# The last tile of an encoder's router on one Trainium2 core: the norm ahead of the row picks, the picks in halves, and another place for the first picked rows

## The reference

```
x = x + concat[GLA(xn), Fourier(xn), MLA(xn)] @ w_out       # xn = rms_norm(x)
t = rms_norm(x)
group = top1(softmax(t @ w_rg + b_rg))                      # 4 groups
two experts = top2(softmax of the 8 logits of that group)   # t @ w_re + b_re, 32 experts
y = sum over the two: weight * (silu(t @ w_gate[e]) * (t @ w_up[e])) @ w_down[e]
return rms_norm(x + y)
```

## Time and profile before

| | |
|---|---|
| median of 3 runs | 531.3 us (530.68 to 532.53) |
| the profiled execution | 531.76 us, span 530.0 us |
| TensorE busy | 493.6 us, 93% of the span, mean granted clock 0.986 |
| VectorE busy | 210.1 us, 40% |
| ScalarE busy | 136.6 us, 26% |
| GpSimd busy | 75.2 us, 14% |
| DMA | 139.95 MB, mean 264 GB/s |
| the chain that ended last | PE 70%, DMA 11%, SPq 8%, DVE 7%, issue 2%, ACT 1% |

### The profile page before, as it was taken

How to read it: one execution, slowest core, us unless ns; L and a number is a source line. 1 busy time by engine, 2 the same in 40 slices (tenths; PEclk the granted TensorE clock), 3 DMA queues, 4 the chain that set the end, 5 groups by cost and what they waited for, 6 DMA issues and landing times.

```text
span 530.0 us, 7702 instructions
## 1 busy us (share of the span) xinstructions
PE 493.6 (93%) x2932; PEld 272.6 (51%) x2932; DVE 210.1 (40%) x561; ACT 136.6 (26%) x357; POOL 75.2 (14%) x101
## 2 busy tenths in 40 slices
PE   4999999999999999999999999999999878788993
PEld 3446544569755555445456555555555434444431
DVE  3217320663576770116763422332233202332166
ACT  4404211362476761203131111111111101111023
POOL 1000000344000000000213122222222212110100
PEclk9999999999999999999998999999999989998998
DMA  8996000010496004941089999999999999999974
GB/s 296 356 279 244 2 1 0 16 36 2 155 416 263 2 1 151 419 144 40 2 307 361 402 420 414 413 419 416 416 414 416 417 415 415 417 415 417 399 288 159
DMA packets 40134, 139.95 MB, mean 264 GB/s; under 512 B 9848, under 2 KB 12984, under 8 KB 31904
## 3 DMA queue, kind: packets, MB, share of 16 engines
q1 hardware_dynamic: 34752, 131.38, 63.1%
q0 software_dynamic: 4816, 7.85, 4.0%
q10 hardware_dynamic: 528, 0.22, 0.2%
HBM read 130.47 MB, written 16.39 MB: 277 GB/s over the span
## 4 chain that ended last, share of the span: by engine, by line
PE 70%; DMA 11%; SPq 8%; DVE 7%; issue 2%; ACT 1%; DVEq 0%; ACTq 0%
PE bank L1063 15%; PE bank L748 12%; DMA EW<-in_moe_w_up 9%; PE bank L928 9%; PE bank L1076 6%; SPq L616 5%; PE bank L911 4%; PE bank L974 3%; PE bank L963 2%; SPq L621 2%; PE bank L845 2%; PE bank L1036 2%; DMA EW<-in_w_in 2%; PE bank L884 1%; PE bank L756 1%
## 5 line engine op out<-in xcount | busy, mean ns | idle before, releaser
L1063 PE MATMUL bank<-EW,WO 128*64 128x256 f32 x640 | 78.3, 400 | 9.8 <-DMA EW<-in_moe_w_up 8.0
L1063 PEld LDWEIGHTS bank<-EW,WO 128*64 128x64 f32 x640 | 47.4, 144 | 35.6 <-DMA EW<-in_moe_w_up 8.8
L748 PE MATMUL bank<-EW,XT 128*128 128x512 f32 (+1 forms) x192 | 64.1, 495 | 0.0
L928 PE MATMUL bank<-WO,XT 128*128 128x512 f32 x128 | 56.6, 595 | 0.0
L1400 ACT ACTIVATE G<-bank 128x128 f32<-128x128 f32 x32 | 8.9, 277 | 178.5 <-PE bank L1063 169.3
L1763 DVE TENSOR_TENSOR G<-G,bank 128x128 f32<-128x128 f32 x32 | 9.2, 287 | 111.7 <-ACT G L1400 93.3
L1988 POOL DMA_INDIRECT y_scratch<-G,sidx x30 | 30.2, 1008 | 162.1 <-DVE G L1776 149.6
L748 PEld LDWEIGHTS bank<-EW,XT 128*128 128x128 f32 x192 | 32.9, 190 | 31.0 <-issue 31.0
L1776 DVE COPY G<-bank 128x512 f32<-128x512 f32 x32 | 22.1, 692 | 47.7 <-PE bank L1076 47.7
L1076 PE MATMUL bank<-EW,G 128*64 128x512 f32 x160 | 38.3, 599 | 0.0
L928 PEld LDWEIGHTS bank<-WO,XT 128*128 128x128 f32 x128 | 23.7, 190 | 27.3 <-issue 27.3
(11 more groups left out here) (291 smaller groups left out, 654.3 us busy)
## 6 DMA issues: line engine op xcount, KB each, us to landing
EW<-in_moe_w_gate SPq DMA_DIRECT2D x20, 1024.0 KB
EW<-in_moe_w_up SPq DMA_DIRECT2D x20, 1024.0 KB
EW<-in_moe_w_down SPq DMA_DIRECT2D x20, 1024.0 KB
y_scratch<-MIX SPq DMA_DIRECT2D x8, 512.0 KB, 9.1
WO<-in_w_out SPq DMA_DIRECT2D x2, 2048.0 KB, 11.7
MIX<-in_moe_w_gate SPq DMA_DIRECT2D x4, 1024.0 KB
MIX<-in_moe_w_up SPq DMA_DIRECT2D x4, 1024.0 KB
WO<-in_moe_w_gate SPq DMA_DIRECT2D x4, 1024.0 KB
```

The lines of the kernel that those rows point to most:

```text
L748: mm = pe.matmul(ps[:, 0:width], xnT[:, c, t * P:(t + 1) * P], w_in_sb[:, c, col:col + width], start=(c == 0), stop=(c == C - 1))
L928: mm = pe.matmul(ps[:, :], xnT[:, c, t * P:(t + 1) * P], w_out_sb[:, c, n * 512:(n + 1) * 512], start=(c == 0), stop=(c == C - 1))
L1063: mm = pe.matmul(bank[BLOCK * m:BLOCK * (m + 1), 0:2 * P].rearrange("p (w n) -> p w n", w=2), xeT[:, c, par * BLOCK:(par + 1) * BLOCK], wv ...
```

## The change

The order of the last steps changes: the norm of tile 3 goes ahead of its logits and of all picks, each pick is split into its two halves, the halves stand before and behind `("Lf", 3)`, `("L", 3)` and `("pos", 3)`. Both filler products are gone. Tile 2's list work leaves its `("pos", 2)` step: the rows are made inside the norm of tile 3, the places after it, and the weights after the selection of tile 3. The two places of gathered rows are exchanged, so that the first picked rows go to the last part of w_out and the first gathered pair to tile 2 of X; VectorE and ScalarE no longer wait for the stores of x. `pick_done` counts halves: VectorE waits for one, ScalarE, SyncE and the first gather for two.

```diff
--- before.py
+++ after.py
@@ -163,8 +163,9 @@
 
 OUT_ORDER = [("out", 0, 0), ("out", 0, 1), ("out", 1, 0), ("T", 0), ("norm", 0), ("out", 1, 1), ("Lf", 0),
              ("out", 2, 0), ("L", 0), ("T", 1), ("norm", 1), ("out", 2, 1), ("Lf", 1), ("pos", 0), ("T", 2), ("norm", 2),
-             ("L", 1), ("out", 3, 0), ("pos", 1), ("Lf", 2), ("L", 2), ("out", 3, 1), ("pos", 2), ("T", 3), ("pick", 0),
-             ("Lf", 3), ("norm", 3), ("L", 3), ("pick", 1), ("pick", 2), ("pos", 3), ("pick", 3)]
+             ("L", 1), ("out", 3, 0), ("pos", 1), ("Lf", 2), ("L", 2), ("out", 3, 1), ("pos", 2), ("T", 3), ("norm", 3), ("pick", 0, 0),
+             ("Lf", 3), ("L", 3), ("pick", 0, 1), ("pick", 1, 0), ("pick", 1, 1), ("pick", 2, 0), ("pos", 3),
+             ("pick", 2, 1), ("pick", 3, 0), ("pick", 3, 1)]
 
 
 def attention_order():
@@ -363,7 +364,7 @@
         hg = view(G, 3840, (2, P))
         hT = view(G, 4096, (2, 2, BLOCK))
 
-        xg = [X[:, 2, :], view(WO, 7168, (D,))]
+        xg = [view(WO, 7168, (D,)), X[:, 2, :]]
         ovx = MIX[:, 0, :]
         yzero = MIX[:, 3, 512:D]
         onehot_held = [MIX[:, i, 0:512].rearrange("p (t d s) -> p t d s", t=T, d=2) for i in range(2)]
@@ -650,7 +651,7 @@
             for t in range(T):
                 drained(sp, ("Lf", t))
             load_gate_up(RING + 2, RING + 2)
-            sp.wait_ge(pick_done, 1)
+            sp.wait_ge(pick_done, 2)
             sp.wait_ge(x2_stored, 16 * T)
             load_down(RING + 2, RING + 2)
             sp.wait_ge(weights_ready, 1)
@@ -728,10 +729,6 @@
                     mm = pe.transpose(banks[PLAN[("xT", c)][0]][:, t * P:(t + 1) * P], X[:, t, c:D:C], ident[:, :])
                     if t == T - 1:
                         close_bank(mm, ("xT", c))
-
-            def keep_busy(ps, data):
-
-                pe.matmul(ps[:, :], ident[:, :], data, start=True, stop=True)
 
             def by_feature(key, col, width):
 
@@ -1007,23 +1004,19 @@
                     ps = open_bank(step)
                     close_bank(pe.matmul(ps[:, 0:NG + NE], lf[t % 2], small[:, STACK:ONE_UP], start=True, stop=True), step)
                 elif kind == "pick":
-                    if t == T - 1:
-                        keep_busy(open_bank(("ids", 1)), X[:, 0, 0:512])
                     pe.wait_ge(sel_ready, 2 * t + 2)
                     drained(pe, ("out", t, 0))
                     drained(pe, ("out", t, 1))
+                    n = step[2]
                     if t == 0:
                         for i in range(T * MH - 3, T * MH):
                             drained(pe, ("S", i))
-                    for n in range(2):
-                        mm = pe.matmul(banks[n][:, :], sel0[:, t].rearrange("p e s -> p (e s)"),
-                                       X[:, t, n * 512:(n + 1) * 512], start=(t == 0), stop=(t == T - 1))
+                    mm = pe.matmul(banks[n][:, :], sel0[:, t].rearrange("p e s -> p (e s)"),
+                                   X[:, t, n * 512:(n + 1) * 512], start=(t == 0), stop=(t == T - 1))
                     if t == T - 1:
                         mm.then_inc(pick_done, 1)
                 elif kind == "pos":
                     ps = open_bank(step)
-                    if t == T - 1:
-                        keep_busy(ps, X[:, 0, 0:512])
                     pe.wait_ge(picks_ready, t + 1)
                     for u in range(t + 1):
                         mm = pe.matmul(ps[:, 0:NE], tri[:, 1 if u < t else 0, :], mska[:, u, :],
@@ -1381,8 +1374,7 @@
 
             act.preload_act_table_set("silu_and_others")
 
-            act.wait_ge(pick_done, 1)
-            act.wait_ge(x2_stored, 16 * T)
+            act.wait_ge(pick_done, 2)
             act.activation(xg[0][:, 512:D], banks[1][:, :], ACT.Copy).then_inc(picked, 1)
             def copy_half(half):
                 for j in range(4):
@@ -1665,6 +1657,28 @@
                 link(dve.reciprocal(wts[:, t, 0:1], sc[:, 8:9]))
                 return dve.tensor_tensor(wts[:, t, 1:2], wts[:, t, 0:1], sc[:, 4:5], ALU.mult)
 
+            def positions(t, ps):
+                link(dve.scalar_tensor_tensor(pos1[:, t], ps[:, 0:NE], 1.0, mska[:, t], ALU.add, ALU.mult))
+                for e in range(2):
+                    dve.tensor_scalar(sel0[:, t, e], slot_no[:, e], pos1[:, t, e:e + 1], rn2[:, t, 2:3],
+                                      ALU.is_equal, ALU.mult).then_inc(sel_ready, 1)
+                dve.tensor_tensor(sel4[:, t].rearrange("p (a u) s -> p a u s", u=2),
+                                  pos1[:, t, 2:6].rearrange("p (a u) -> p a u", u=2).unsqueeze(3).to_broadcast([P, 2, 2, BLOCK]),
+                                  slot_no.unsqueeze(1).to_broadcast([P, 2, 2, BLOCK]),
+                                  ALU.is_equal).then_inc(sel4_ready, 1)
+
+            def list_rows(t, ps):
+                step = ("pos", t)
+                row, rows2 = rt[:, t, 10], rt[:, t, 11:13]
+                free_bank(dve.tensor_tensor(row, ps[:, 0:NE], small[:, 0:NE], ALU.add), step)
+                drained(dve, step)
+                link(dve.tensor_tensor(rows2, oh[:, t], row.unsqueeze(1).to_broadcast([P, 2, NE]), ALU.mult))
+
+            def list_places(t):
+                link(dve.tensor_reduce(rt[:, t, 0, 10:12], rt[:, t, 11:13], AX, ALU.add))
+                dve.scalar_tensor_tensor(dest[:, t, :], rt[:, t, 0, 10:12], -1.0, rt[:, t, 0, 10:12],
+                                         ALU.mult, ALU.max).then_inc(dest_ready, 1)
+
             for step in OUT_ORDER:
                 kind, t = step[0:2]
                 if kind == "out":
@@ -1679,8 +1693,12 @@
                     dve.tensor_scalar(rn2[:, t, 1:2], rn2[:, t, 0:1], rn2[:, t, 4:5], EPS, ALU.add, ALU.add).then_inc(var_ready, 1)
                     norms[0] += 1
                     dve.wait_ge(var_ready, norms[0])
+                    if t == T - 1:
+                        list_rows(t - 1, banks[PLAN[("pos", t - 1)][0]])
                     refine(rn2[:, t, 2:3], rn2[:, t, 1:2], rn2[:, t, 3:4])
                     dve.tensor_copy(lrow[:, t, :, 1], rn2[:, t, 2:3].to_broadcast([P, 2])).then_inc(row_ready, 1)
+                    if t == T - 1:
+                        list_places(t - 1)
                 elif kind == "T":
                     if t == T - 1:
                         ps = filled(dve, ("x2T", t, 1))
@@ -1704,33 +1722,22 @@
                     link(first_max(l32, NE, t, 9, oh[:, t, 1], sc[:, 7:8]))
                     dve.tensor_tensor(mska[:, t], oh[:, t, 0], oh[:, t, 1], ALU.add).then_inc(picks_ready, 1)
                     dve.tensor_tensor(sc[:, 5:6], sc[:, 7:8], sc[:, 6:7], ALU.subtract).then_inc(logit_ready, 1)
+                    if t == T - 1:
+                        link(weights(t - 1))
                 elif kind == "pos":
                     ps = filled(dve, step)
-                    link(dve.scalar_tensor_tensor(pos1[:, t], ps[:, 0:NE], 1.0, mska[:, t], ALU.add, ALU.mult))
-                    for e in range(2):
-                        dve.tensor_scalar(sel0[:, t, e], slot_no[:, e], pos1[:, t, e:e + 1], rn2[:, t, 2:3],
-                                          ALU.is_equal, ALU.mult).then_inc(sel_ready, 1)
-                    dve.tensor_tensor(sel4[:, t].rearrange("p (a u) s -> p a u s", u=2),
-                                      pos1[:, t, 2:6].rearrange("p (a u) -> p a u", u=2).unsqueeze(3).to_broadcast([P, 2, 2, BLOCK]),
-                                      slot_no.unsqueeze(1).to_broadcast([P, 2, 2, BLOCK]),
-                                      ALU.is_equal).then_inc(sel4_ready, 1)
-                    row, rows2 = rt[:, t, 10], rt[:, t, 11:13]
-                    free_bank(dve.tensor_tensor(row, ps[:, 0:NE], small[:, 0:NE], ALU.add), step)
-                    drained(dve, step)
-                    link(dve.tensor_tensor(rows2, oh[:, t], row.unsqueeze(1).to_broadcast([P, 2, NE]), ALU.mult))
-                    link(dve.tensor_reduce(rt[:, t, 0, 10:12], rows2, AX, ALU.add))
-                    dve.scalar_tensor_tensor(dest[:, t, :], rt[:, t, 0, 10:12], -1.0, rt[:, t, 0, 10:12],
-                                             ALU.mult, ALU.max).then_inc(dest_ready, 1)
-
-                    if t < T - 1:
-                        link(weights(t))
+                    positions(t, ps)
+                    if t != T - 2:
+                        list_rows(t, ps)
+                        list_places(t)
+                        if t < T - 1:
+                            link(weights(t))
             def copy_tokens(pair):
                 dve.wait_ge(xe_full, 2 * pair + 1)
                 dve.tensor_tensor(xeT[:, 0:4], banks[0][:, :].rearrange("p (j s) -> p j s", j=4),
                                   gain2[:, 0:4].unsqueeze(2).to_broadcast([P, 4, P]), ALU.mult).then_inc(xe_ready, 1)
 
             dve.wait_ge(pick_done, 1)
-            dve.wait_ge(x2_stored, 16 * T)
             dve.tensor_copy(xg[0][:, 0:512], banks[0][:, :]).then_inc(picked, 1)
```

(2 more changed lines are left out.)

## The result

| | before | after |
|---|---|---|
| median of 12 runs each, us | 531.34 (529.65 to 533.97) | 533.17 (531.93 to 534.04) |
| ratio, 95% interval | 1 | 1.0039 [1.0026, 1.0052] |
| profiled execution, us (span) | 531.76 (530.0) | 533.29 (531.5) |

A forecast was written before the change was run, and what follows sets the result against it. The weight stream was taken as the bound, so TensorE's gain counts only by filling a hole. 531.76 less 1.0 gives 530.8; 0.46 lower for the median gives 530.3, said as 530.2; range 528.4 to 532.4 us.

The forecast's parts named there:

- the places come after the norm: VectorE, tile 2's list work: places follow tile 3's norm (ends 269.3), done at 269.7, before the logits at 269.82.
- X<-w_down is issued at 279.1: SyncE's queue: this load still waits for x_scratch's last store, landing at 279.03, so goes at 279.1 instead of 279.62.
- G<-w_down is issued 4.2 us before the queue runs dry, so it should follow without a hole: SyncE's queue: issue at 281.8 instead of 283.53, 4.2 us ahead against 2.5, closes the 286 us hole; 1.0 us.
- the hole stays: Rival: the 286 us hole has another cause, such as the two gathers; time 531.2 us, chance 0.20.
- TensorE's 1.75 us: TensorE before the experts: earlier logits and picks move the first gate/up from 282.85 to 281.1.
- The selection is unchanged: VectorE, last tile: selection takes as long as before, so the last positions product (L1029) starts at 274.04 instead of 275.67.
- Slower: Rival: without fillers TensorE falls to half clock on the picks, about 1.56 us a stretch; 533.1 us, chance 0.12.
- Clearly faster: Rival: the late half-clock product after a weight wait runs at full clock, 1.67 us more; 528.6 us, chance 0.21.
- 1.0 us of stream: DMA weight stream: gain from closing the hole at 286 us, 0.89 and a little of its slope; bounds 0 and 1.75.

The follow-up runs named there:

- e6: Kernel before, with only tile 2's list scatters waiting longer, until the last tile's row is ready: 533.78 us, 1.0054 of before.
- e7: Kernel after with tile 2's list rows and places back behind its selection matrices, only its weights still late: 530.20 us, 0.9986 of before.
- e2: Kernel after, with tile 3's store to x_scratch issued ahead of the five weight loads that follow the out product: 531.49 us, 1.0007 of before.
- e1: Kernel after, unchanged, run again for a second trace: 534.23 against 531.32 us, 1.0052 of before.
- e4: Kernel after, with the XT gate and up loads issued behind the last logits' scaling instead of their copy: 534.42 us, 1.0059 of before.
- e9: Kernel before without the last tile's two list scatters, so its tokens are missing in the lists: 527.15 against 530.68 us, 0.9921.
- e12: Kernel after with tile 2's list rows and places back behind its selection matrices, weights still late, 5 rounds: 530.43 us, 0.9988 of before.
- e5: Kernel after, with tile 2's two list scatters waiting until tile 3's places are there too: 533.84 us, 1.0066 of before.
- e3: Kernel before, with only the last x_scratch store issued ahead of the weight loads: 531.31 us, 0.9999 of before.
- e8: Kernel before, with tile 2's two list scatters waiting until tile 3's places are there too: 534.70 us, 1.0069 of before.
- e10: Kernel after with tile 2's list rows and places back in its positions step, ahead of its selection matrices: 530.47 us, 0.9983 of before.
- e11: Kernel after with tile 2's list rows and places back behind its selection matrices, and the last x_scratch store ahead of the loads: 529.99 us, 0.9978.

## Why the prediction was wrong

**The step that failed: "the places come after the norm".** It was costed on VectorE alone, 0.4 us ahead of the logits, and there it was right. But `dest` releases GpSimd's scatters, and these were never priced: the prediction names no row of GpSimd, and its sum has no term for them. What they cost by going out later: e6 is the kernel before with nothing but later scatters (3.7 us), 1.0054; e7 is the kernel after with the scatters back at their old time, 0.9986 instead of 1.0052. The forecast was 530.2 for 531.3, 0.998. Both together show that the scatters' place in time makes the difference between the forecast and the result, to within the intervals.

**"X<-w_down is issued at 279.1".** It was issued at 282.23, since the store landed at 282.2. The store's landing was carried over from before (279.03), and the change itself moved it; e2 gets back nearly all of the loss by making the landing early. The Trainium skill (DMA: Bandwidth & Descriptors, "Queues, rings and completion order") says that a DMA's semaphore increment on an engine lands only after every earlier write of that engine, whichever queue it came from. The traces agree as far as they go. In after, e1 and e4 the scatters' packets moved and the stall began before the store was in, and it landed at the stall's end (14.8, 15.0 and 15.8 us after its issue). In e6 only 15 of the pair's packets had moved by 278 us, the store landed at 277.9 (10.8 us), and the stall came behind it. Which engine's write held the increment back, no run shows.

**"G<-w_down is issued 4.2 us before the queue runs dry, so it should follow without a hole".** The hole was real, its cause wrong. In rows 5 the window at 285 had a share of 1.37 at 267 GB/s, the sign of packets that hang, which I gave to the gathers as a rival; e9 puts it down to tile 3's scatters. The rival "the hole stays" had the right doubt and the wrong culprit. That the hole is smaller in e7 (328 GB/s over 285 to 287 us, in e12, the same program, 242, before 156) was therefore not earned by G<-w_down's issue, and why it is smaller was not separated.

**TensorE's 1.75 us** came out at 1.28 in the kernel after. The logits are on time (269.88), but the last positions product started at 274.43, not 274.04. "The selection is unchanged" was not quite so. VectorE in the kernel before, then after:

```profile
272.49 0.23 DVE L1659 TENSOR_SCALAR G<-G 128x4 f32<-128x4 f32 x1
```

```profile
270.87 0.51 DVE L1651 TENSOR_SCALAR G<-G 128x4 f32<-128x4 f32 x1
```

The same instruction takes 0.28 us more, and ends at 271.38, when GpSimd's first scatter (270.42 + 0.97) ends. In e1 and e2 it took 0.51 as well and ended with the scatter again (in e2 both at 270.56); in e5 and e7, where no scatter runs beside it, 0.23. So the moved scatters seem to reach VectorE too; the other 0.1 us was not traced. In e7 the first gate/up is at 281.70, 1.15 us before that of the earlier trace rows.

**The rivals.** "Slower" was priced at 533.1 us and 533.17 was measured, but that is luck: its half-clock stretches did not happen where they were put. The granted clock stayed at 1.00 up to 281 us without the fillers, in after and in e7. In the kernel after the half-clock product is another one (297.65, 5.58 us), behind the wait of 2.43 us for the lists; in e7, which waits 0.8 us for them, it is absent. The first gate/up at half clock, 1.56 us of its own, is no fixed cost either: with the fillers it was there before and in e9, and not in e3, e6 and e8; without them only e2 has it. "Clearly faster" was over-priced. The late product at half clock (5.34 us in the earlier trace rows) ran at full clock in the kernel after:

```profile
482.86 3.67 PE L1056 MATMUL bank<-EW,WO 128*64 128x256 f32 x32 [1.94 <-DMA EW<-in_moe_w_up]
```

It is at half clock in four of the fourteen traces (before, e5, e10, e12), and e7 and e12 are one program, so it changes from execution to execution. From last w_up to the end of the span it is 72.6 to 72.8 us in these four and 71.9 to 72.1 in the other ten: worth 0.7 us, not 1.67. This 0.7 us is why 2.2 us of stream showed as 1.5 in the profiled executions.

**The size of the gain** was about right once the scatters are apart: 1.0 us of stream was forecast, e7's last w_up is 0.86 us earlier than before (456.47 against 457.33) and its median 0.45 us lower, e12's 0.25 us. That agreement is partly luck, since the hole's cause was wrong. The bound of the kernel (the weight stream, and TensorE waiting for up weights late) held: in all fourteen traces TensorE stood 1.7 to 1.9 us for the up weight issued last on the chain, and where last w_up moved by over 2 us (to 454.96 in e9, to 459.51 to 460.65 in after, e1, e4, e5 and e6), the time moved the same way.

**What stays open.** What holds the engines after such writes; and why tile 2's pair costs almost nothing when its packets move in 272 to 276 us (before, e7), amid loads and a store that run at 309 GB/s anyway, and brings a stall of 2 to 3 us when they move 2 to 5 us later, while with the store ahead the early place has a stall too (e3, 191 GB/s over 3 us; e11).

## What to carry to other kernels

When an instruction moves, look up every semaphore that it increments and price what that releases on each other engine, GpSimd's indirect DMAs first: here a shift of 2 us of two scatters of 1 KB each cost more than the whole change was forecast to bring. In a stream that is full, read the DMA share beside the GB/s: a low rate at a share near or over 1 is a stall of open packets; a low share may be a dry queue, or the tail of such a stall, as in rows 5. Then count: bytes issued less bytes moved tells whether there was anything to move. A time taken from the trace for a DMA's landing holds only as long as nothing that shares the engines with it is moved.

## What was unexpected of the hardware

The scatters of one tile are 256 writes of 8 bytes, 64 packets and 1.2% of the engines' time in the queue's row. They can be followed by several us in which all 16 engines together move far less than 417 GB/s: 202 over 5 us in the kernel after, 180 over 4 us in e6, and 142 over 6 us behind four scatters in e5. In the kernel after, the stall behind 2 KB of scatters has the length of 1.1 MB of weights (2.6 us at 417 GB/s). And a store of half a MB in SyncE's queue landed after 2.9 (e3), 3.6 (e2), 10.8 (e6), 11.7 (before), 15.0 (e1) or 15.8 us (e4), by what stood ahead of it and what ran beside it.
